# Block 1 of the modulation summed by TensorE alone, and fewer throw-away matmuls

## The reference

```python
c_act = jax.nn.silu(c)                       # (1, 1024)
mod = c_act @ w_ada[l] + b_ada[l]            # (1, 6144)
sh1, sc1, g1, sh2, sc2, g2 = jnp.split(mod, N_MOD, axis=-1)
h = modulate(rms_norm(x, norm1_w[l]), sh1, sc1)     # h * (1 + sc1) + sh1
mix = hybrid_mixer(h, w_in[l], ...)
```

## Time and profile before

| | us |
|---|---|
| median of 3 runs | 912.92 (912.11 to 915.02) |
| the profiled execution | 913.21 |
| its span, first to last instruction | 911.4 |
| TensorE busy | 883.0 |
| VectorE busy | 668.6 |
| ScalarE busy | 504.4 |

### The profile page before, as it was taken

How to read it: one execution, slowest core, us unless ns; L and a number is a source line. 1 busy time by engine, 2 the same in 40 slices (tenths; PEclk the granted TensorE clock), 3 DMA queues, 4 the chain that set the end, 5 groups by cost and what they waited for, 6 DMA issues and landing times.

```text
span 911.4 us, 18632 instructions
## 1 busy us (share of the span) xinstructions
PE 883.0 (97%) x8020; PEld 839.3 (92%) x8020; DVE 668.6 (73%) x1132; ACT 504.4 (55%) x814; POOL 65.7 (7%) x83
## 2 busy tenths in 40 slices
PE   5998999999999999999999999999999999999997
PEld 1797898999898989999999999999888999999997
DVE  3878867566979687677888884678666778888653
ACT  2489667453344637655355444456665567666442
POOL 0100201121001101020000000220000200000011
PEclk9999999999999999999999999999999999999999
DMA  8755332333776664464998889635332536555631
GB/s 334 262 195 185 99 134 97 137 139 97 245 261 229 234 232 165 165 216 183 273 339 300 280 287 262 229 116 192 139 138 92 182 140 214 203 185 177 249 130 47
DMA packets 27681, 177.31 MB, mean 195 GB/s; under 512 B 2864, under 2 KB 5680, under 8 KB 7504
## 3 DMA queue, kind: packets, MB, share of 16 engines
q1 hardware_dynamic: 27600, 176.13, 55.6%
HBM read 174.29 MB, written 1.84 MB: 193 GB/s over the span
## 4 chain that ended last, share of the span: by engine, by line
PE 81%; DVE 8%; ACT 6%; DMA 2%; POOL 1%; issue 1%; SPq 0%; DVEq 0%; ACTq 0%
PE ps L1093 45%; PE ps L1099 22%; PE ps L1091 2%; DVE wl L1841 2%; ACT wh L1454 2%; PE ps L1138 1%; DVE acc L1740 1%; PE ps L1146 1%; PE ps L1232 1%; PE ps L1149 1%; PE ps L1097 1%; PE ps L1252 1%; DMA raw<-in_ada_dram 1%; DMA raw<-in_w_in_dram 1%; DVE KT L1723 1%
## 5 line engine op out<-in xcount | busy, mean ns | idle before, releaser
L1841 DVE TENSOR_TENSOR wl<-raw,wh 128x1024 fp32r<-128x1024 f32 x265 | 321.4, 1232 | 75.1 <-ACT wh L1454 74.4
L1093 PE MATMUL ps<-HH,wh 128*128 128x256 f32 x1480 | 369.5, 286 | 0.7 <-ACT HH L1428 0.2
L1093 PE MATMUL ps<-HH,wl 128*128 128x256 f32 x1480 | 356.4, 277 | 0.0
L1454 ACT ACTIVATE wh<-raw 128x1024 fp32r<-128x1024 f32 x265 | 273.3, 1042 | 140.0 <-PE ps L1099 107.5
L1093 PEld LDWEIGHTS ps<-HH,wh 128*128 128x128 f32 x1480 | 278.8, 188 | 9.4 <-issue 4.3
L1093 PEld LDWEIGHTS ps<-HH,wl 128*128 128x128 f32 x1480 | 278.4, 188 | 1.9 <-issue 1.9
L1099 PE MATMUL ps<-HL,wh 128*128 128x256 f32 x1480 | 225.9, 277 | 0.0
L1099 PEld LDWEIGHTS ps<-HL,wh 128*128 128x128 f32 x1480 | 194.7, 188 | 0.1
L1093 PE MATMUL ps<-FH,wl 128*128 128x256 f32 x352 | 84.5, 276 | 0.0
L1093 PE MATMUL ps<-FH,wh 128*128 128x256 f32 x352 | 84.5, 276 | 0.0
L1740 DVE SCALAR_TENSOR_TENSOR acc<-raw,silc,acc 128x512 f32<-128x512 f32 x101 | 76.3, 756 | 8.1 <-DMA raw<-in_ada_dram 5.0
(11 more groups left out here) (269 smaller groups left out, 1088.9 us busy)
## 6 DMA issues: line engine op xcount, KB each, us to landing
raw<-in_ada_dram SPq DMA_DIRECT2D x32, 1024.0 KB, 5.6
raw<-in_w_fi_dram SPq DMA_DIRECT2D x22, 1024.0 KB, 4.9
raw<-in_w_up_dram SPq DMA_DIRECT2D x22, 1024.0 KB, 4.8
raw<-in_w_rest_dram SPq DMA_DIRECT2D x20, 1024.0 KB, 4.8
raw<-in_w_in_dram SPq DMA_DIRECT2D x16, 1024.0 KB, 4.8
raw<-in_w_qkv_dram SPq DMA_DIRECT2D x12, 1024.0 KB, 4.8
raw<-in_w_o_dram SPq DMA_DIRECT2D x8, 1024.0 KB, 4.9
raw<-in_w_fo_dram SPq DMA_DIRECT2D x8, 1024.0 KB, 5.0
```

The costliest lines, as they stand in the source:

```text
L1093: e.matmul(o, w[:, k, 128 * t:128 * t + 128], x_hi[:, k0 + k, :], start=first and n + k == 0, **MM)
L1454: e.activation(whl[u % HALF][0][:, 0:n], raw[i % RAW][:, c:c + n], ACT.Copy).then_inc(*a_hi.up(u))
L1841: e.tensor_tensor(wl[:, 0:n], raw[i % RAW][:, c:c + n], wh[:, 0:n].bitcast(F32), ALU.subtract).then_inc(*v_lo.up(u))
```

## The change

Block 1's second item is summed as rows too. So block 1 needs no accumulation, no transposes, no reduction and no second sum on VectorE; the turn of block 1 now writes its final value. The turn is started only after the second item. The throw-away matmuls go from 16 to 6 and from 10 to 8.

```diff
-        ada_item(b, kp, rows=b == 0 or (b, kp) == (1, 0))
+        ada_item(b, kp, rows=b < 2)
...
-            if b == 1 or kp == 1:
+            if kp == 1:
                 tasks.append(ada_turn(b, rows_bank[0]))
...
-        while b == 1 and ("turn", 1, 1) not in made:
-            yield
...
-        until(*((("turn", n, 1) if n == 0 else ("red", n, 1)) for n in (2 * b, 2 * b + 1)))
+        until(*((("turn", n, 1) if n < 2 else ("red", n, 1)) for n in (2 * b, 2 * b + 1)))
...
-            for _ in range(10):
+            for _ in range(8):
                 e.matmul(o[:, 0:128], ones, eye, start=True, **MM)
...
-                    for _ in range(16):
+                    for _ in range(6):
                         e.matmul(psum[b][:, 0:128], ones, eye, start=True, **MM)
...
-        if b == 1:
-            v_misc.wait_ge(e, "turn", 1)
```

More of the change, by code:

```diff
@@ L1747, in dve_reduce @@
         col = modc[:, 4 * b:4 * b + 4]
-        bias = col if b == 1 else v("b_ada", 4 * b, 4) if b < 12 else v("b_ada_f", 4 * (b - 12), 4)
+        bias = v("b_ada", 4 * b, 4) if b < 12 else v("b_ada_f", 4 * (b - 12), 4)
         p_misc.wait_ge(e, "red", b)
@@ L1869, in vector_engine @@
                 ins = e.tensor_tensor(modc[:, 4 * blk:4 * blk + 4], psum[b][:, 0:4], v("b_ada", 4 * blk, 4), ALU.add)
-                ins.then_inc(*v_misc.up(*(("mod", 0) if blk == 0 else ("turn", 1))))
-                if blk == 0:
-                    v_misc.at[("turn", 0)] = v_misc.at[("mod", 0)]
+                ins.then_inc(*v_misc.up("mod", blk))
+                v_misc.at[("turn", blk)] = v_misc.at[("mod", blk)]
             elif kind == "red" and ev[2] == 1:
```

## The result

The changed kernel took 922.22 us (median of 4 runs, 920.83 to 927.49) beside 913.08 (912.11 to 915.02) for the kernel before: a ratio of 1.0092, interval 1.0054 to 1.0130, so slower by 8 to 9 us. I had forecast 913.1 with a range up to 916.4. The profiled execution spans 919.0 us instead of 911.4.

What follows compares the result with a forecast made beforehand. TensorE's instruction stream plus its waits was taken as the bound (busy 883.0 of 911.4 us). Beginning +1.0 and mixer -1.0 summed to 0, giving 913.1 us, range 910.3 to 916.4.

Steps and rivals of the forecast that it cites:

- 1.2 us of chain: Beginning: the new string of steps after the last piece lands starts the first weight split 1.2 us later.
- the slack of 0.2: Beginning: the second unit's low parts were ready 0.2 us before use; the delay uses this up, TensorE 1.0 us later.
- the heads' steps move by two tiles: Mixer: fewer startup turns put every head's steps two output tiles earlier, a tile being 1.36 us.
- the walk through head 0: Mixer, head 0: TensorE waits 1.6 us at the key tile; qg, near 83.6, comes before TensorE asks, replacing a 2.8 wait.
- For head 1 the same walk gives a wait of about 1.7: Mixer, head 1: TensorE's wait becomes about 1.7 us where 0.9 stood.
- rival 1: Beginning: the clock falls in the new gap, about 32 us, slowing row matmuls by some 1.7 us; 914.8, chance 0.2.
- the head of 281.22: Mixer: its 1.58 us wait behind an accumulation on VectorE becomes 0.9, a gain of 0.7.
- The 1.3 at L1155: Mixer: TensorE's wait for a VectorE step behind a split; between 0 and 1.3 us saved, taken as -0.6.
- new waits elsewhere: Rest of the mixer: none to 3.1 us, taken as +0.7 because VectorE and ScalarE have room to catch up.
- waits of heads 0 and 1: Mixer: the two heads' waits together 3.3 us against 3.7 before, a gain of 0.4.
- Rival 3: Mixer slower: heads' steps meet a convolution or accumulation ahead on VectorE; +3.5 us in all, 916.6, chance 0.12.
- The upper bound of +3 for the mixer: Mixer: top of the range -4 to +3 around the forecast sum of -1.0 us.

Runs made afterwards that it cites:

- e1: The changed kernel with one added to the tick counter after startup: new beginning, mixer heads' steps in their old place; ratio 1.0036 to the kernel before.
- e10: e3 with the block of Silu and Square passes of the second pair of tiles put behind the exponentials of heads 0 and 1; ratio 1.0143.
- e3: The changed kernel with a shortened beginning (six throw-away matmuls dropped, block 3's transposes ahead of block 1's turn) and heads in the old place; ratio 0.9977.
- e4: The changed kernel with two added to the tick counter, a third place of the heads' steps; ratio 1.0060.
- e6: The changed kernel with heads 0 and 1 in their old place and heads 2 to 7 in the new one; ratio 1.0006.
- e2: The kernel before with one taken off the tick counter after startup: old beginning, heads' steps where the changed kernel has them; ratio 1.0054.
- e5: The changed kernel with heads 2 to 7 back in their old place, heads 0 and 1 in the new one; ratio 1.0065.
- e7: The changed kernel with the Silu block before head 1's exponential copying instead, so without its two table loads; changes what is computed; ratio 1.0053.
- e9: e3 with 16 throw-away matmuls ahead of head 0's wait for qg, which overran it; ratio 1.0015.
- e11: The changed kernel with 12 throw-away matmuls ahead of head 1's wait for qg, which fit into it; ratio 1.0055.
- e12: e3 with 8 throw-away matmuls ahead of head 0's wait for qg, which fit into it; ratio 0.9974.
- e8: The changed kernel with 24 throw-away matmuls ahead of head 1's wait for qg, which overran it; ratio 1.0074.

## Why the prediction was wrong, step by step

**The beginning was right.** First split 38.97 forecast, 38.85 in e1; TensorE's idle time before the second row matmuls 1.6 forecast, 1.52 measured; 1.2 us of chain forecast, 1.16 against its own first row matmuls in the changed kernel, a lag of 1.09 in e1. TensorE's stream was forecast 1.0 us later. The low parts of the second unit were awaited for 0.33 us, since the slack of 0.2 was used up, as forecast. Eight throw-away matmuls instead of ten cost nothing.

**That the heads' steps move by two tiles was right,** and so was the walk through head 0: a wait of 1.64 at the key tile (1.6 forecast), none at L1117, qg at 83.14 (83.6).

**The step that failed first is the sentence "For head 1 the same walk gives a wait of about 1.7".** It measured 3.87 in place of 0.89, 2.2 us more than forecast. The walk followed VectorE's queue and TensorE's arrival, and not ScalarE's: once head 0's qg stands ahead of the Silu block, its lc stands behind it, and lc holds up VectorE, which holds k of head 1. Head 0's waits went from 2.80 to 1.64 us, and head 1's grew by 2.98. The price of the table load back to the exponential, 1.28 us, belongs to it too: in the old place the load at 86.81 stands ahead of head 0's qg, and both heads' exponentials follow it.

**The second failure is the clock.** In my terms it belonged to the beginning alone, with rival 1 for a fall at 32 us. It did not fall there. It fell behind head 1's wait, and cost 1.7 us there. I had no term for a fall in the mixer, though a longer wait was among my own bounds.

**The remaining terms:** at the head of 281.22 a wait of 0.9 was forecast, 0.45 measured. The 1.3 at L1155 was to shrink by 0.6, to 0.7; it is gone at that place, since the step now stands ahead of the split, as forecast, but two steps further TensorE waits for y:

```profile
322.06 1.28 ACT L1592 ACT_TABLE_LOAD   x1
323.35 2.01 ACT L1592 ACTIVATE ZS<-ZS 128x1024 f32<-128x1024 f32 x2
...
326.33 0.27 ACT L1369 ACTIVATE y<-ps 64x128 f32<-64x128 f32 x1
```

```profile
326.65 0.44 PE L1158 MATMUL ps<-inv,y 64*64 64x64 f32 x4 [1.70 <-ACT y L1369]
```

Again ScalarE, with a table load and passes ahead of a 0.27 us copy. And "new waits elsewhere", put at +0.7 with the argument that the engines are only 73% and 55% busy, came to 3.7 us: 1.12 at 138.76, 0.51 at 147.75, 1.62 at 193.06 (no more than 0.17 before) and 0.46 at 244.90 (in place of 0.70 near there), or 2.8 net of the small old waits. The mean share of busy time says nothing of a queue at one moment; that argument was the weakest of the sum.

**The account** of the mixer, in the prediction's terms:

| | forecast | measured |
|---|---|---|
| waits of heads 0 and 1 | -0.4 | +1.8 |
| wait of the head at 281.22 | -0.7 | -1.1 |
| wait at L1155, now for y | -0.6 | +0.4 |
| new waits elsewhere | +0.7 | +2.8 |
| the clock's fall | no term | +1.7 |
| TensorE's slower pace | no term | +2.0 |
| sum | -1.0 | 7.6 of 8.0 |

TensorE's waits grew from 7.6 to 11.5 us, by 3.9. The 0.4 us left over are not resolved. So the walk of head 1 and the term for new waits are each 2.1 to 2.2 us too low, and 3.7 us have no term at all.

**The rivals.** Rival 3 had the sign and put the mixer at +2.5, by a step that meets a pass on VectorE; what came was three times as large, and its largest wait was decided on ScalarE. The upper bound of +3 for the mixer was one accumulation of VectorE and held no term for ScalarE's five passes with two table loads, though the block stood in the trace of before, ahead of qg at 88.10.

## What to carry to other kernels

A change that alters a count or a turn in the planner moves every later step that goes by it; separate the two effects with one line before judging the work itself. When steps of two chains share in-order queues, walk *every* queue that a step passes, ScalarE's with its table loads as well as VectorE's, and for each step that moves ahead of a block ask which sibling now stands behind it. Filling a wait with throw-away work can pay only where it fits into the wait and where no later wait lets the clock fall anyway; no run here is shown to have kept more than 0.4 us of what it gave back. When waits and clock do not add up to the loss, count matmuls in equal stretches in which TensorE has no wait.

## What the runs showed of the hardware

In the traces the granted clock fell once between 20 and 900 us in nearly all of these kernels, and took the same time in all but one fall (in e10, twice as long): two stretches of 3 us at 0.92 and 0.51 before the change, 0.71 and 0.72 behind the wait at 93.97 after it; both add up to 3.4 us at the lower level, 1.7 us of TensorE's work. What a change of the kernel did was to move it: from the beginning (the kernel before) to the wait of head 0 (e1, e3, e4, e6) or head 1 (the change, e2, e5), and with these waits shortened or filled to the waits near 320 us (e7, e9, e11, e12). In e6 it came once more, near 27 us, and in e10 four times. e11 measures its price as 1.65 us. One trace is one execution: the mean granted clock of the changed kernel's four executions was 0.993, 0.995, 0.997 and 0.997, so in two of the three without a trace TensorE spent more time at the lower level. In e8 it did not come at all (mean granted clock 0.999), though the same wait of 1.7 us for y stands there; so whether such a wait lets it fall is not settled by the wait alone. The Trainium skill ("TensorE: Matmul & The Clock Gate", Part 1) says that the throttled clock is the default and activity releases it, and that the number of throttled matmuls at a kernel's start varies between runs of one kernel. The traces agree with both: the same first eight records took 6.38 us before and 5.04 in the changed kernel, and those at 25.52 took 3.60. By the rule alone I had looked for the danger where filler was taken away, at 32 us, and it was in a wait 60 us later.

TensorE has a second, slower pace that the granted clock does not show: product matmuls start 0.113 or 0.118 us apart at a granted clock of 1.00, in stretches of up to 184 us. It took 2.1 us from 355 to 405 us with the later heads in the new place and 6.9 us in e2 from 729 us on. Of the 35 executions of the kernel before beside e1 to e4, 25 lie from 911.4 to 917.3 us and 10 from 918.5 to 923.0; such a stretch would be enough for the difference, but none of the ten has a trace.
